# Two encoder layers on one core: the S5 recurrence computed by blocks of four tokens instead of token by token

## The reference, cut to what matters

```python
D_MODEL = 1024; SEQ = 256; DEPTH = 2; D_FF = 2816
D_A = D_B = 384; D_C = 256; C_GROUP = 16; C_GROUPS = 16; C_STATE = 64; B_HEADS = 6
# each of the two layers
#   x <- LN(alpha*x + 0.5*SwiGLU_1(x))                                    FFN1
#   x <- LN(alpha*x + W_out[ RMS(RG-LRU) | RMS(attention) | RMS(S5+GLU) ]) mixer
#   x <- LN(alpha*x + 0.5*SwiGLU_2(x))                                    FFN2
def s5_ssm(u, a_re, a_im, log_dt, b_re, b_im, c_re, c_im, d, w_glu):
    lam = lax.complex(a_re, a_im); dt = jnp.exp(log_dt)[:, None]
    a_bar = jnp.exp(lam * dt)                                # (16 groups, 64 states)
    b_bar = ((a_bar - 1.0) / lam)[:, :, None] * lax.complex(b_re, b_im)
    ug = u.reshape(bsz, s, C_GROUPS, C_GROUP)
    bu = jnp.einsum('bsgc,gpc->bsgp', ug, b_bar)
    h = linear_scan(a_seq, bu)                               # h_t = a_bar * h_(t-1) + bu_t
    y = jnp.einsum('bsgp,gcp->bsgc', h, c_mat).real + d * ug
    y = jax.nn.gelu(y)
    return y * jax.nn.sigmoid(y @ w_glu)
def hybrid_mixer(x, w_in, ...):
    z = x @ w_in             # a_x 384, a_gate 384, q 384, k 384, v 384, f_logit 6, c_u 256
    ...                      # RG-LRU of a_x gated by gelu(a_gate); attention of q, k, v with
    ...                      # forget gates f_logit; s5_ssm of c_u; each RMS-normed, then w_out
```

## Time and profile before

| what | value |
|---|---|
| median of 3 runs | 1113.58 us (1111.46 to 1116.91) |
| profiled execution: own time, span | 1108.28 us, 1106.5 us |
| granted TensorE clock, mean | 0.962 |
| PE busy | 1040.1 us, 94% of the span |
| PEld busy | 941.5 us, 85% |
| DVE busy | 691.0 us, 62% |
| ACT busy | 477.1 us, 43% |
| POOL busy | 338.0 us, 31% |
| HBM | 176.43 MB, 159 GB/s |

### The profile page before, as it was taken

How to read it: one execution, slowest core, us unless ns; L and a number is a source line. 1 busy time by engine, 2 the same in 40 slices (tenths; PEclk the granted TensorE clock), 3 DMA queues, 4 the chain that set the end, 5 groups by cost and what they waited for, 6 DMA issues and landing times.

```text
span 1106.5 us, 17091 instructions
## 1 busy us (share of the span) xinstructions
PE 1040.1 (94%) x6894; PEld 941.5 (85%) x6894; DVE 691.0 (62%) x792; ACT 477.1 (43%) x540; POOL 338.0 (31%) x374
## 2 busy tenths in 40 slices
PE   7999999889987999999889999999899879999997
PEld 7999999766776999999788999998677769999996
DVE  5575754798668745454676666458975687454456
ACT  4544444432683444344354344335226733444441
POOL 2159900275330600000071797004661415000000
PEclk9999999988998999999989999999889889999999
DMA  9755466431214565565456556553312146555541
GB/s 287 236 191 189 159 206 193 126 115 39 115 33 159 195 195 180 190 189 191 154 149 220 190 186 193 190 172 99 111 38 115 54 137 229 191 187 190 192 153 38
DMA packets 135265, 176.43 MB, mean 159 GB/s; under 512 B 10317, under 2 KB 119593, under 8 KB 135209
## 3 DMA queue, kind: packets, MB, share of 16 engines
q1 hardware_dynamic: 133432, 169.33, 47.8%
q0 software_dynamic: 1728, 6.29, 1.5%
q10 hardware_dynamic: 48, 0.02, 0.0%
HBM read 174.56 MB, written 1.05 MB: 159 GB/s over the span
## 4 chain that ended last, share of the span: by engine, by line
PE 76%; DVE 12%; issue 4%; POOL 3%; ACT 3%; DMA 0%; DVEq 0%; POOLq 0%; ACTq 0%
PE bank L1422 24%; PE bank L1423 24%; PE bank L1424 23%; DVE wlo L904 2%; DVE bn L1109 1%; ACT whi L574 1%; POOL gin L524 1%; DVE xT_f L1126 1%; PE bank L1620 1%; DVE xT_lo L1158 1%; PE bank L1619 1%; DVE xtok L1107 1%; DVE xtok L1089 1%; POOL hh L530 1%; POOL osq L543 1%
## 5 line engine op out<-in xcount | busy, mean ns | idle before, releaser
L904 DVE TENSOR_TENSOR wlo<-raw,whi 128x2048 fp32r<-128x2048 f32 x157 | 393.3, 2507 | 286.4 <-ACT whi L574 285.8
L1422 PE MATMUL bank<-xT_hi,whi 128*128 128x256 f32 x1632 | 474.2, 291 | 13.7 <-DVE xT_lo L1158 12.3
L1423 PE MATMUL bank<-xT_lo,whi 128*128 128x256 f32 x1632 | 469.4, 288 | 0.0
L1424 PE MATMUL bank<-xT_hi,wlo 128*128 128x256 f32 x1632 | 469.1, 287 | 0.0
L1422 PEld LDWEIGHTS bank<-xT_hi,whi 128*128 128x128 f32 x1632 | 321.4, 197 | 22.5 <-DVE xT_lo L1158 13.4
L574 ACT ACTIVATE whi<-raw 128x2048 fp32r<-128x2048 f32 x157 | 299.0, 1906 | 87.8 <-PE bank L1424 84.1
L1423 PEld LDWEIGHTS bank<-xT_lo,whi 128*128 128x128 f32 x1632 | 321.6, 197 | 1.5
L1424 PEld LDWEIGHTS bank<-xT_hi,wlo 128*128 128x128 f32 x1632 | 320.9, 197 | 0.0
L1422 PE MATMUL bank<-whi,act_hi 128*128 128x512 f32 x416 | 165.8, 399 | 0.0
L1423 PE MATMUL bank<-wlo,act_hi 128*128 128x512 f32 x416 | 165.1, 397 | 0.0
L1424 PE MATMUL bank<-whi,act_lo 128*128 128x512 f32 x416 | 164.3, 395 | 0.0
(11 more groups left out here) (262 smaller groups left out, 937.9 us busy)
## 6 DMA issues: line engine op xcount, KB each, us to landing
raw<-in_ffn_w_up SPq DMA_DIRECT2D x44, 1024.0 KB, 5.4
raw<-in_ffn_w_down SPq DMA_DIRECT2D x44, 1024.0 KB, 5.0
raw<-in_ffn_w_gate SPq DMA_DIRECT2D x43, 1024.0 KB, 5.4
raw<-in_w_in SPq DMA_DIRECT2D x18, 1024.0 KB, 5.3
raw<-in_w_out SPq DMA_DIRECT2D x8, 1024.0 KB, 6.1
lngb<-in_ln_g POOLq DMA_DIRECT2D x6, 512.0 KB, 5.2
lngb<-in_ln_b POOLq DMA_DIRECT2D x6, 512.0 KB, 6.6
xtok<-in_x SPq DMA_DIRECT2D x2, 512.0 KB, 4.7
```

The costliest lines, as they stand in the source:

```text
L904: V.tensor_tensor(wlo[:, s, 0:n], raw[:, s, 0:n], whi[:, s, 0:n].bitcast(F32), ALU.subtract)\
L1422: T.matmul(out, a_hi, b_hi, start=first, stop=False)
L1423: T.matmul(out, a_hi, b_lo, start=False, stop=False)
L1424: return T.matmul(out, a_lo, b_hi, start=False, stop=last)
```

## The change

S5 is computed by blocks of four tokens (`BLK = 4`, 64 blocks, `NBLK`). A block's inputs, 4 tokens by 32 channels, fill the 128 partitions of `u4`. For each of the 8 tiles one pair of matmuls (`s5_inputs`) gives what the block adds to the state at its end; the scan then goes over 64 blocks, and since the decay row `dec` is zero at the start of each tile, one scan of 512 covers all 8 tiles of one part. Three matmuls a tile (`s5_outputs`) give the four tokens' outputs: one of the block's own inputs by `kst` (the response within a block, with the skip term on its diagonal), two of the state at the end of the block before, by powers of the transition times C (`cpow`). All of them have 64 columns and accumulate in bank 2.

The matrices are made in FFN1. POOL multiplies B by the transition three times (`bpow`) and C four times (`cpow`), 18 and 24 operations of 128x256, and its doublings now go to 64 columns only (6 of them, the last on 128x256). PE turns C's four matrices (4 transposes) in the second pair, and in the last pair but one turns `bpow` (16 transposes, `inputs_turned`) and forms the responses (`responses`, 16 float32 matmuls of 32x128). ACT evacuates: `cpow` 2 of 128x256, `bst` 4 of 128x512, `ksb` 2 of 32x512, and 4 copies of 32 rows into `kst`. DVE adds the skip term once (`skip_terms`). For this, banks 5 and 7 are free: every gate piece goes to bank 4, every up piece to bank 6, and PE waits for `silu_done` ahead of a gate piece and for `hid_done` ahead of an up piece.

In the mixer ACT builds `u4` with 16 instructions of 32x128 (`blocks_in`) and takes the outputs through the Gelu with another 16 (`blocks_out`), in place of one of 128x512; `s5_sum`, the 8 transposes, their evacuations and POOL's 32 additions go. DVE does the eight turns and two scans of all tiles in 10 instructions. The order of the pieces is now values, values, u, a_x, a_x and gate, three pieces that each hold 128 columns of q and 128 of k (two loads of half a piece), gates; what depends on them is moved in each engine's program. `scores(4)`, `scores(5)` and `values(3)` now stand behind the first half of `project_s5`.

```diff
-ZPIECES = [4 * DA, 4 * DA + PC, NIN - DC, 3 * PC, 4 * PC, 5 * PC, 0, PC, 2 * PC]
+ZPIECES = [4 * DA, 4 * DA + PC, NIN - DC, 0, PC, None, None, None, 2 * PC]
...
+                for b in range(BLK - 1, 0, -1):
+                    old, new = slice(b * CH, (b + 1) * CH), slice((b - 1) * CH, b * CH)
+                    times_a(bpow[:, 0, :, old], bpow[:, 1, :, old], bpow[:, 0, :, new], bpow[:, 1, :, new], 1)
+                for b in range(BLK):
+                    times_a(cpow[:, 0, :, b, :], cpow[:, 1, :, b, :], cpow[:, 0, :, b + 1, :], cpow[:, 1, :, b + 1, :], -1)
...
-                while n < SEQ:
+                while n < NBLK:
...
+                def blocks_in():
+                    z_wait(5)
+                    src = bank[z_bank(4)].rearrange("p (q j s) -> p q j s", q=2, s=BLK)
+                    for i in range(4):
+                        for b in range(BLK):
+                            A.activation(u4[b * CH:(b + 1) * CH, i::4, 1:], src[i * CH:(i + 1) * CH, :, :, b], ACT.Copy)\
+                                .then_inc(u4_ready, 1)
+                def blocks_out():
+                    ...
+                            A.activation(dst[i * CH:(i + 1) * CH, :, :, b], src[b * CH:(b + 1) * CH, :, i, :],
+                                         ACT.Gelu_apprx_tanh).then_inc(ys_gelu, 1)
...
+                    s5step(V.tensor_tensor(s5_t[:, 0:2, :], banks[:, 2:4, :], cosines, ALU.mult))
+                    s5step(V.tensor_tensor(s5_t[:, 2:4, :], banks[:, 2:4, :], sines, ALU.mult))
+                    s5step(V.tensor_tensor(gin[:, 0, :], s5_t[:, 0, :], s5_t[:, 3, :], ALU.add))
+                    s5step(V.tensor_tensor(gin[:, 1, :], s5_t[:, 1, :], s5_t[:, 2, :], ALU.subtract))
...
+                        s5step(V.tensor_tensor_scan(s5_t[:, r, :], decay, gin[:, r, :], 0.0, ALU.mult, ALU.add))
...
-                    pe.wait_ge(ly.hid_done, n)
-                    features(g, i * 6, 4 + par_)
-                    features(u, i * 6, 6 + par_)
+                    mats = f == 0 and isinstance(i, int) and q == 0
+                    pe.wait_ge(ly.silu_done, n + 1)
+                    if mats:
+                        inputs_turned(0)
+                    features(g, i * 6, 4)
+                    pe.wait_ge(ly.hid_done, n + 1)
+                    features(u, i * 6, 6)
+                    if mats:
+                        inputs_turned(2)
+                        responses()
...
+                def s5_inputs():
+                    for i in range(S5_TILES):
+                        for r in range(2):
+                            ins = T.matmul(banks[:, 2 + r, i * NBLK:(i + 1) * NBLK], bst[:, r, i, :], u4[:, i, 0:NBLK],
+                                           start=True, stop=True)
+                def s5_outputs():
+                    for i in range(S5_TILES):
+                        dst, j = bank[2][:, i * NBLK:(i + 1) * NBLK], slice(i * NBLK, (i + 1) * NBLK)
+                        T.matmul(dst, kst[:, i, :], u4[:, i, 1:], start=True, stop=False)
+                        for r in range(2):
+                            ins = T.matmul(dst, cpow[:, r, i, 1:, :].rearrange("p b c -> p (b c)"), s5_t[:, r, j],
+                                           start=False, stop=r == 1)
```

More of the change, by code:

```diff
@@ L87 @@
 F_V_DONE = 17
+S5_V_DONE = 10
 XTOK_SCALED = (2, 8, 14)
@@ L180, in trunk @@
         squared = (gs, osq, ig)
-        bank = [ps(f"bank{i}") for i in range(8)]
+        banks = ctx.enter_context(nc.psum_tensor("bank", [P, 8, 512], F32))
+        bank = [banks[:, i, :] for i in range(8)]
         def sem(name):
@@ L246, in loaded @@
         def loaded(L, pos0, step, turns):
-            done = sum(slot(q) == slot(pos0) for q in range(pos0 + 1))
-            return (L * SLOT_USES[slot(pos0)] + turns + done) * 16
+            done = sum(loads(q) for q in range(pos0 + 1) if slot(q) == slot(pos0))
+            return (L * SLOT_LOADS[slot(pos0)] + turns + done) * 16
         gate_w = [w[f"ffn{f}_w_gate"].rearrange("l (k p) (j n) -> l j p k n", p=P, n=PC) for f in (1, 2)]
@@ L595, in ffn_pair @@
                     last = isinstance(i, int) and i > 0
+                    mats = last and f == 0
                     g, u, d = pair_pos(f, q)
@@ L772, in _ @@
                 values_out(0)
+                ahead(1)
                 values_out(1)
-                ahead(1)
-                for n, (r, dst) in enumerate(((7, bT), (6, cT))):
-                    act.wait_ge(bc_turned, 2 * L + n + 1)
-                    A.activation(dst[:, :, :].rearrange("p a n -> p (a n)"), bank[r][:, :], ACT.Copy)\
-                        .then_inc(bc_ready, 1)
                 ahead(2)
-                evac(4, uT[:, 0, :])
-                evac(5, uT[:, 1, :])
                 act.wait_ge(ly.f_v, 1)
@@ L806, in _ @@
+                blocks_out()
                 attn_exp(0)
-                evac(11, kT[:, 2, :])
-                ahead(6)
+                evac(14, qT[:, 2, :], scale=HD ** -0.5)
                 attn_exp(1)
-                evac(12, ax[:, 0, 3:])
+                evac(15, kT[:, 2, :])
                 attn_turn(0)
-                conv_tap(0)
-                evac(13, ax[:, 1, 3:])
-                conv_tap(1)
+                ahead(7)
+                decays()
+                act.wait_ge(ly.decay_done, 3)
@@ L949, in ffn_pair @@
                         input_scales()
+                    if last and f == 0 and q == 0:
+                        skip_terms()
                 def ffn(f):
@@ L1792, in _ @@
                 values(2)
                 turn_probs(3)
-                glu()
-                z_event(17)
-                values(3)
-                scores(5)
                 square_sums(0, 2, 0)
                 project_s5((0, 1))
+                values(3)
+                scores(4)
+                scores(5)
+                project_s5((2, 3))
                 turn_probs(4)
-                project_s5((2, 3))
                 values(4)
```

536 lines of the change are left out of this document (298 added, 238 removed).

## The result

The changed kernel takes 1144.1 us (median of 4 runs, 1133.99 to 1146.1) against 1113.84: 1.026 of the kernel before, interval 1.020 to 1.032. On another chip, beside the experiments, it was 1.020 (1.016 to 1.023). Forecast were 1112 us and a range of 1098 to 1127.

A forecast was written before the change was run, and what follows sets the result against it. PE was taken as the bound, with no slack in FFN1 and some 12 us a mixer. Per layer +7.4 in FFN1 and -8.0 in the mixer made -0.6, -1.2 for two: 1112 us, range 1098 to 1127.

The forecast's parts named there:

- FFN1, +7.4 us: FFN1, per layer: added transposes 2.2 us, response matmuls 4.0, wait for ACT 1.2; range 6.5 to 12.
- Rival D: FFN1: POOL finishes the matrices late and PE stands still, +5 to +15 us a layer, 1130 us; chance 0.03.
- The list of matmuls up to z_event 17, -10.1 us: Mixer, per layer: 17.2 us of PE work goes, 10.0 comes, and scores(4) with values(2), 2.9 us, move later.
- rival B: FFN1 and mixer: small float32 matmuls cost 0.42 us instead of 0.25, 19 us for both layers, 1131 us; chance 0.09.
- New waits: Mixer up to z_event 17: PE waits 1.2 us for u4 and 4 us behind ACT's queue, taken as 5.
- so does most of the low clock: Mixer up to z_event 17: half-clock stretches beside the S5 chain go if PE runs on, 6 us a layer.
- old waits: Mixer up to z_event 17: PE's waits for POOL and DVE in the old S5 chain go, 7.4 us a layer.
- The end of the mixer: From z_event 17 on: 16.5 us to the end of scores(5), formerly 6; mixer ends 8 us earlier (3 to 13).
- ACT's stretch: Mixer, from the end of s5_outputs to S5's high halves: 24 us of ACT's queue, level with PE's 27 us.
- rival C: Mixer: ACT's queue takes over, PE idles, gain 3 instead of 8 us a layer; +9 us, 1121 us; chance 0.19.

The follow-up runs named there:

- v_conv_first: Changed kernel with queues reordered, small u4 and Gelu pieces shared between ACT and DVE, DVE's conv(1) ahead of its low half: 1088.93 us, ratio 0.979.
- a_again: The changed kernel once more, unaltered, on the chip of three further experiments: 1136.66 us, ratio 1.020 to the kernel before.
- v_order_only: Changed kernel with only the order of its queues altered, all 32 small ACTIVATEs still on ACT: 1098.27 us, ratio 0.986 to the kernel before.

## Why the prediction was wrong

**FFN1, +7.4 us: right.** It is 7.3 us in both layers (169.3 instead of 162.0 from the parameters' transpose to the first z_event). Eight transposes 1.04 us, responses 3.65 us (expected 4.0; 0.23 us each), the wait for ACT 1.24 (expected 1.2). Rival D, late matrices, did not happen. The low end of the range given there should be 5.9 by its own parts, not 6.5, and the parts of the whole sum, all on one side, give 1100 to 1130, not 1101 to 1124; neither changes what follows.

**The list of matmuls up to z_event 17, -10.1 us: right in size where the clock is full.** At full clock `s5_outputs` takes 5.3 us for 24, 0.22 us a matmul where the sum had 0.25, so rival B is out. In the runs of the changed kernel they were mostly not at full clock.

**"New waits", 5 us, and "so does most of the low clock", 6 us: the step that failed.** Up to z_event 17 the sum was 10.1 of matmuls + 7.4 of old waits + 6 of low clock - 5 of new waits = 18.5 us. From first to last z_event the changed kernel gained 6.0 us in layer 0 and 5.0 in layer 1. The same stretch in the kernel before, in the changed kernel and in v_conv_first, layer 0:

```profile
205.20:309.00 103.80, 95.17 (x583) 76.76 (x583) 75.10 (x126) 44.81 (x80) 53.06 (x48) 0.93 0.28 92
211.70:309.40 97.70, 86.25 (x573) 78.32 (x574) 57.51 (x83) 50.97 (x106) 21.01 (x14) 0.90 0.31 94
212.20:293.90 81.70, 78.36 (x574) 71.46 (x574) 60.39 (x110) 45.85 (x87) 21.88 (x16) 0.98 0.35 105
```

The old waits went, but new ones of 3.2, 2.4, 3.2 and 1.4 us came up to z_event 15, 10.2 us where the sum had 5.2, and PE's idling rose from 8.6 to 11.5 us instead of falling. The low clock was tied to the S5 chain; it came back behind the new waits, 0.90 instead of 0.93, so that PE's busy time fell by 8.9 us and not by 10.1 and 6. The third row tells that the two gains were there to be had: with the queues put in order PE idles 3.3 us, at clock 0.98, and z_event 17 comes 22 us earlier after the mixer's start than in the kernel before.

**The end of the mixer.** From z_event 17 to the end of `scores(5)` it is 18.3 us in both layers (16.5 forecast, 6.1 before). The wait ahead of `project_s5` is 2.4 us after one of 1.1 (3 forecast). ACT's stretch from the end of `s5_outputs` (271.8) to S5's high halves (317.5) is 46 us, not 24: the sum took ACT as if it never waited, and it waits for z_event 13, for logits and for `attn_out(0)`. That is rival C, held at 0.19 and priced at +9 us in all; it came at +26, since C left the forecast of z_event 17 as it was. The projections behind are as before.

So by the spans +6.5 and +7.3 us for the two FFN1 (7.3 in both from the parameters' transpose on) and +5.5 and +6.6 for the mixers, where the forecast had +7.4 and -8.0: 26 us. What the order of the queues is worth, with the same S5, the ladder shows: a_again 1.020, v_order_only 0.986, v_conv_first 0.979. In v_conv_first the mixers are 127.2 and 129.3 us, 18 us shorter than before, and FFN1's cost is the only loss of the change that is left. The 8 us a layer that were forecast for the mixer so were within reach of the new S5, but not of the changed kernel's queues. The forecast had the parts on PE right, and took from the trace of before how long each engine needs, but not whom each would wait for in the new order.

Left open: why z_event 16 of layer 0 runs at 0.50 even where the wait ahead of `glu` is filled, when that of layer 1 does not; waits of 1.4 and 0.9 us and the scores lie between. And why the profiled run of the changed kernel, 1133.99 us at clock 0.951, is 10 us faster than its others at 0.937 to 0.943; layer 0's `s5_outputs` at 0.86 and layer 1's at 0.50 in one execution show the two ways, but what decides between them no run tells.

## What to carry to other kernels

Before a chain is taken off the path, leave most of it out and time what remains: a single run gives an estimate of the gain with its waits, here 19 us a layer of which 14 were matmuls. It can be too low, since what remains can still be waited for (7.1 us here). Where an in-order queue gets new work, add up the waits that stand ahead of it and not only its own time: leaving the 32 small ACTIVATEs out gave 1.1 to 1.7%, sharing them with another queue gave nothing, and putting the queues in another order, with all 32 still on ACT, gave 3.4%. A wait of 2.7 us on PE cost 6.8 us more in half clock behind it, so a queue is first cleared of the waits that stand ahead of dense matmuls, and where that can't be done idle matmuls in the gap are worth trying.

## What the runs showed of the hardware

Behind a wait of 2.7 us the clock was 0.51 for 15.1 us; behind the same time filled with matmuls it was 1.00. In the kernel before the layer norm behind the first mixer has waits of 3.3 and 4.4 us, and FFN2 begins at half clock before it runs at full speed:

```profile
360.60:364.60 4.00, 4.00 (x19) 4.00 (x20) 3.23 (x1) 2.54 (x2) 3.84 (x2) 0.50 0.00 0
```

The Trainium skill, "TensorE: Matmul & The Clock Gate", section "HAM oscillation — how this bites in real kernels", describes a low clock that follows idleness. The runs agree in these places. They do not tell when it follows: the waits ahead of `gates(1)`, 2.4 us in layer 0 and 1.8 in layer 1 of one execution, were followed by 0.86 and 0.50. The same page, section "What's actually happening", says of a kernel's start that the number of slow matmuls differs between runs of one kernel. The spread here is in the middle of a kernel, and no run shows its cause.

An ACTIVATE of 32x128 took 0.29 us as a copy and 0.41 us through the Gelu (16 in 4.67 and 6.59 us), both from PSUM, both with a stride of four on one side; the sum had 0.25. DVE's copies of the same shape took 0.32 from PSUM (8 in 2.55 us) and 0.30 from SBUF.
